# Splitting the first gate's load into idle homes, finer release of buffers, and TensorE's branch turned about

## The reference

```python
h = h + (g_a * y_a + g_b * y_b) @ w_out[l]
hn = rmsnorm(h, norm_ffn_g[l])
# top-1 of 4 groups, then top-2 of the 8 experts in it; combine has 2 weights per token
for e in range(N_EXPERTS):
    h_e = jax.nn.silu(xf @ w_gate[e]) * (xf @ w_up[e])      # 1024 -> 512
    y = y + combine[:, e:e + 1] * (h_e @ w_down[e])         # 512 -> 1024
return rmsnorm(h + y, norm_final_g)
```

## Time and profile before

| what | value |
|---|---|
| median of 3 timed runs | 902.14 us (901.19 to 902.33) |
| profiled execution | 902.81 us |
| its span | 901.07 us |
| granted TensorE clock, mean | 0.979 of full |
| TensorE busy | 853.9 us, 95% |
| DMA | 250.53 MB, mean 278 GB/s |
| chain that ended last | PE 83%, DMA 11%, DVE 3% |

### The profile page before, as it was taken

How to read it: one execution, slowest core, us unless ns; L and a number is a source line. 1 busy time by engine, 2 the same in 40 slices (tenths; PEclk the granted TensorE clock), 3 DMA queues, 4 the chain that set the end, 5 groups by cost and what they waited for, 6 DMA issues and landing times.

```text
span 901.1 us, 11362 instructions
## 1 busy us (share of the span) xinstructions
PE 853.9 (95%) x4613; PEld 551.7 (61%) x4613; DVE 426.4 (47%) x827; ACT 218.8 (24%) x400; POOL 7.5 (1%) x23
## 2 busy tenths in 40 slices
PE   8999999999999999999999967999996799999976
PEld 7888888877777888888734323443542353644632
DVE  5538325677675344436768242434333324335123
ACT  6322222564543222223211111100110100100114
POOL 0000000000000100000000000000000000000000
PEclk9999999999999999999999978999998899999999
DMA  8544212212123733794899999999999999999995
GB/s 296 148 95 117 94 47 94 94 48 94 48 94 84 214 107 94 275 404 162 326 363 420 421 427 425 427 408 423 429 413 428 429 427 426 428 428 426 428 412 198
DMA packets 70887, 250.53 MB, mean 278 GB/s; under 512 B 22792, under 2 KB 46384, under 8 KB 56880
## 3 DMA queue, kind: packets, MB, share of 16 engines
q1 hardware_dynamic: 70320, 248.18, 70.6%
q0 software_dynamic: 432, 1.57, 0.6%
q10 hardware_dynamic: 80, 0.02, 0.0%
HBM read 245.56 MB, written 4.20 MB: 277 GB/s over the span
## 4 chain that ended last, share of the span: by engine, by line
PE 83%; DMA 11%; DVE 3%; issue 1%; ACT 1%; SPq 0%; DVEq 0%; POOLq 0%
PE bank L976 17%; PE bank L670 9%; PE bank L671 9%; PE bank L672 9%; PE bank L1033 8%; DMA R<-w_down 7%; DMA R<-w_gate 3%; PE bank L697 2%; PE bank L698 2%; PE bank L699 2%; PE bank L942 2%; PE by_side L942 2%; PE bank L1020 2%; PE bank L1061 1%; PE bank L1062 1%
## 5 line engine op out<-in xcount | busy, mean ns | idle before, releaser
L976 PE MATMUL bank<-R,packT 128*64 128x512 f32 (+1 forms) x972 | 187.1, 609 | 13.9 <-DMA R<-w_up 7.9
L976 PEld LDWEIGHTS bank<-R,packT 128*64 128x64 f32 (+1 forms) x972 | 59.2, 129 | 123.5 <-issue 122.9
L1544 DVE TENSOR_TENSOR wlo<-raw,whi 128x2048 fp32r<-128x2048 f32 x33 | 75.5, 2287 | 85.2 <-ACT whi L1226 84.7
L670 PE MATMUL bank<-xnT_hi,whi 128*128 128x512 f32 x288 | 113.6, 395 | 0.0
L672 PE MATMUL bank<-xnT_hi,wlo 128*128 128x512 f32 x288 | 112.2, 389 | 0.0
L671 PE MATMUL bank<-xnT_lo,whi 128*128 128x512 f32 x288 | 112.1, 389 | 0.0
L1033 PE MATMUL bank<-R,actT 128*64 128x512 f32 (+1 forms) x384 | 76.0, 653 | 15.3 <-DMA R<-w_down 15.1
L1226 ACT ACTIVATE whi<-raw 128x2048 fp32r<-128x2048 f32 x33 | 63.0, 1909 | 69.0 <-PE by_side L672 33.8
L1033 PEld LDWEIGHTS bank<-R,actT 128*64 128x64 f32 (+1 forms) x384 | 22.9, 137 | 63.3 <-issue 62.6
L672 PEld LDWEIGHTS bank<-xnT_hi,wlo 128*128 128x128 f32 x288 | 54.1, 188 | 11.5
L670 PEld LDWEIGHTS bank<-xnT_hi,whi 128*128 128x128 f32 x288 | 54.1, 188 | 11.3 <-issue 0.6
(11 more groups left out here) (392 smaller groups left out, 1318.2 us busy)
## 6 DMA issues: line engine op xcount, KB each, us to landing
R<-w_up SPq DMA_DIRECT2D x26, 2048.0 KB, 19.6
R<-w_gate SPq DMA_DIRECT2D x25, 2048.0 KB, 20.1
R<-w_down SPq DMA_DIRECT2D x21, 2048.0 KB, 19.4
raw<-w_in SPq DMA_DIRECT2D x17, 1024.0 KB, 5.2
R<-w_down SPq DMA_DIRECT2D x13, 1024.0 KB, 14.4
R<-w_gate SPq DMA_DIRECT2D x9, 1024.0 KB, 7.4
R<-w_up SPq DMA_DIRECT2D x7, 1024.0 KB, 11.0
raw<-w_in SPq DMA_DIRECT2D x20, 256.0 KB, 4.5
```

The lines of the kernel that those rows point to most:

```text
L670: pe.matmul(dst, hi_w, hi_x, start=start, stop=False)
L976: mm = pe.matmul(dst[s * w:(s + 1) * w, :], packT[:, side, c, s * w:(s + 1) * w], part_of(s, c) if part_of else slots[s // 2].tiles[s % 2] ...
L1544: dve.tensor_tensor(wlo[c % 2][:, :], raw[c % 2][:, :], whi[c % 2][:, :].bitcast(F32), ALU.subtract).then_inc(lo_split, 1)
```

## The change

Four things, with no change of what is computed.

1. `first_gate` shrinks to blocks 4 to 7 (8 KB at 16). Blocks 0 and 1 get `gate_head` (4 KB at 214), block 2 `gate_third` (2 KB at 196), block 3 `gate_fourth` (2 KB at 209.5). Some of the router's temporaries change places so that the last one is free in time.
2. Expert 2's up matrix is loaded whole into `R[0]` where half of it was.
3. The releases become finer: after each of the blocks 0 to 5 of the first gate, and after 1, 2, 4 and 6 blocks of the first up projection. The reads of `order` are spread over SP's program.
4. TensorE's program is turned about: the case without overflow is the first branch and holds the whole rest; the case with overflow holds the overflow loop and a second copy of the rest. Round 3's gate waits for one add instead of all; the banks of that spread are taken in another order (bank 0 first); the wait for all adds moves behind the gate.

```diff
-    first_gate = at("first_gate", [P, 8 * DE], F32, 8)
+    first_gate = at("first_gate", [P, 4 * DE], F32, 16)
+    gate_head = at("gate_head", [P, 2 * DE], F32, 214)
+    gate_third = at("gate_third", [P, DE], F32, 196)
+    gate_fourth = at("gate_fourth", [P, DE], F32, 209.5)
...
+        GATE_FIRST = ((0, 2, 3, 5), (6, 7, 1, 2))
+            return GATE_FIRST if line is main and i == OVER_AT - 1 else SPREAD_BANKS
...
-        FIRST_LOADED = (48, 32, 32, 48)
+        FIRST_LOADED = (96, 32, 32, 48)
+        GATE_PARTS = [(c, c + 1) for c in range(6)]
+        UP_PARTS = ((0, 1), (1, 2), (2, 4), (4, 6), (6, 8))
...
-            sp.dma_start(first_gate[:, :], flat(w_gate, 0)).then_inc(slot_loaded[0], 16)
+            sp.dma_start(first_gate[:, :], flat(w_gate, 0)[:, 4 * DE:8 * DE]).then_inc(slot_loaded[0], 16)
             sp.dma_start(first_down[0][:, :], flat(w_down, 0)[:, 0:4 * DE]).then_inc(slot_loaded[2], 16)
-            sp.dma_start(R[0][:, 0:4 * DE], flat(w_up, 2)[:, 0:4 * DE]).then_inc(up_ahead, 16)
+            sp.dma_start(R[0][:, :], flat(w_up, 2)).then_inc(up_ahead, 16)
...
+            sp.wait_ge(hsq_summed, 2 * TT)
+            sp.dma_start(gate_head[:, :], flat(w_gate, 0)[:, 0:2 * DE]).then_inc(slot_loaded[0], 16)
             sp.wait_ge(logits_done, TT)
+            sp.dma_start(gate_third[:, :], flat(w_gate, 0)[:, 2 * DE:3 * DE]).then_inc(slot_loaded[0], 16)
             sp.dma_start(R[6][:, :], flat(w_gate, 2)).then_inc(slot_loaded[3], 16)
+            sp.wait_ge(masks_ready, 1)
+            sp.dma_start(gate_fourth[:, :], flat(w_gate, 0)[:, 3 * DE:4 * DE]).then_inc(slot_loaded[0], 16)
             sp.wait_ge(row_token_ready, 2)
             sp.dma_start(first_down[1][:, :], flat(w_down, 0)[:, 4 * DE:8 * DE]).then_inc(spare_loaded, 16)
...
-            sp.wait_ge(gate_half_done, 1)
-            load_part(4, 0, w_up, 2, 4, 6)
-            load_part(5, 0, w_down, 2, 0, 2)
-            sp.wait_ge(gate_half_done, 2)
-            load_part(4, 0, w_up, 2, 6, 8)
-            load_part(5, 0, w_down, 2, 2, 4)
+            def load_behind_gate(c0, c1):
+                sp.wait_ge(gate_half_done, c1)
+                load_part(5, 0, w_down, 2, c0, c1)
+            for c0, c1 in GATE_PARTS[0:2]:
+                load_behind_gate(c0, c1)
             sp.wait_ge(ordered, 1)
-            quad = [ordered_expert(n) for n in range(4)]
+            quad = {1: ordered_expert(1)}
+            for c0, c1 in GATE_PARTS[2:4]:
+                load_behind_gate(c0, c1)
+            quad[0] = ordered_expert(0)
+            for c0, c1 in GATE_PARTS[4:]:
+                load_behind_gate(c0, c1)
+                load_part(6, 1, w_gate, quad[1], c0 - 4, c1 - 4)
             sp.wait_ge(main.gate_done, 1)
-            load_part(5, 0, w_down, 2, 4, 6)
-            load_part(6, 1, w_gate, quad[1], 0, 4)
...
+            load_part(6, 1, w_gate, quad[1], 2, 4)
+            for n, (c0, c1) in enumerate(UP_PARTS):
+                if c1 < KT:
+                    sp.wait_ge(up_half_done, n + 1)
+                else:
+                    sp.wait_ge(main.up_done, 1)
+                load_part(5, 1, w_down, 3, c0, c1)
+                load_part(6, 0, w_gate, quad[0], c0, c1)
+            quad |= {n: ordered_expert(n) for n in (2, 3)}
             sp.wait_ge(down_half_done, 1)
...
-                    if half_done is not None and (c == KT // 2 - 1 or finer and c == KT // 4 - 1):
+                    if half_done is not None and c + 1 in halves:
...
-                        pe.wait_ge(line.h_added, 8 * i + 1)
+                        pe.wait_ge(line.h_added, 8 * i + spread_banks(line, i)[0].index(2) + 1)
...
+            for i in range(OVER_AT):
+                run_round(i)
+            n_over = pe.value_load(ov_count[0:1, 0:1], min_val=0, max_val=OV_TILES)
+            pe.wait_ge(main.pack_a, 4)
+            pe.wait_ge(main.pack_b, 4)
+            for n in range(2):
+                spread(main, OVER_AT - 1, n, 1 - OVER_AT % 2)
+            def run_rest():
+                pe.wait_ge(main.h_added, 8 * (OVER_AT - 1) + 1)
+                for i in range(OVER_AT, LAST):
+                    run_round(i)
+                finish()
+            with pe.If(n_over < 1):
+                run_rest()
+            with pe.Else():
+                run_overflow()
+                run_rest()
...
+                dve.wait_ge(gate_half_done, 2)
                 make_weights(main, spaced_iota, 0)
```

More of the change, by code:

```diff
@@ L983, in first_gate_part @@
             def first_gate_part(s, c):
-                tile = first_gate if s == 0 else R[1] if c < 6 else gate_rest
-                c = c - 6 if tile is gate_rest else c
-                return tile[:, c * DE:(c + 1) * DE]
+                if s == 0:
+                    tile, c0 = (gate_head, 0) if c < 2 else (gate_third, 2) if c == 2 else (gate_fourth, 3) if c == 3 else (first_gate, 4)
+                else:
+                    tile, c0 = (R[1], 0) if c < 6 else (gate_rest, 6)
+                return tile[:, (c - c0) * DE:(c - c0 + 1) * DE]
             def turn_weights(line, odd):
@@ L1094, in _, with run_round @@
                 turn_fetched(0, n, 2 + n)
-            for i in range(LAST):
+            def run_round(i):
                 odd = i % 2
                 side = odd if i > 2 else 0
[L1098 to L1118, removed]
-                        gather_rows(over, OV_PAIRS // 2 + 1)
-                        pe.wait_ge(over.pack_a, OV_PAIRS + 2)
-                        pe.wait_ge(over.pack_b, OV_PAIRS + 2)
-                    pe.wait_ge(main.h_added, 8 * i)
-                elif i >= 2:
+                if i >= 2 and i != OVER_AT:
                     pe.wait_ge(main.h_added, 8 * (i - 1))
@@ L1132, in _ @@
                     number_rows(2, 2)
-                project(main, slots_of(i, 1), side, bank[1], main.up_done, half_done=up_half_done if i < 2 else None, finer=True)
+                project(main, slots_of(i, 1), side, bank[1], main.up_done, half_done=up_half_done if i < 2 else None,
+                        halves=[c1 for _, c1 in UP_PARTS[:-1]] if i == 0 else (2, 4))
                 if i == 1:
@@ L1166, in _ @@
                     gather_rows(main, i // 2 + 1)
-            last, odd = LAST, LAST % 2
-            pe.wait_ge(main.h_added, 8 * (last - 1))
-            project(main, slots_of(last, 0), odd, bank[0], main.gate_done, packed=None if odd else last + 1)
-            turn_weights(main, odd)
-            for k in range(KT):
-                mm = pe.matmul(bank[1 if k < 4 else 4][:, (k % 4) * P:(k % 4 + 1) * P],
-                               final_gT[:, k:k + 1].to_broadcast([P, P]), ident[:, :], start=True, stop=True)
@@ new lines, in run_overflow @@
+            def run_overflow():
+                pe.wait_ge(main.h_added, 8 * OVER_AT)
+                with pe.Fori(0, OV_PAIRS // 4) as j:
+                    for q in range(4):
+                        o, odd = 4 * j + q, q % 2
+                        if not odd:
+                            gather_rows(over, 2 * j + (q // 2 + 1))
+                        project(over, over_slot(j, q, 0), odd, bank[0], over.gate_done, packed=None if odd else o + 1)
+                        turn_weights(over, odd)
+                        project(over, over_slot(j, q, 1), odd, bank[1], over.up_done)
+                        turn_rows(over, o)
+                        project_down(over, over_slot(j, q, 2), o, None)
+                        for n in range(2):
+                            spread(over, o, n, odd)
+                        pe.wait_ge(over.h_added, 8 * o + 8)
+                gather_rows(over, OV_PAIRS // 2 + 1)
+                pe.wait_ge(over.pack_a, OV_PAIRS + 2)
+                pe.wait_ge(over.pack_b, OV_PAIRS + 2)
@@ L2028, in add_rows @@
                         part = h_tok[:, t, n * 512:(n + 1) * 512]
-                        dve.tensor_tensor(part, bank[SPREAD_BANKS[n][t]][:, :], part, ALU.add).then_inc(line.h_added, 1)
+                        dve.tensor_tensor(part, bank[spread_banks(line, i)[n][t]][:, :], part, ALU.add).then_inc(line.h_added, 1)
             def copy_right(r, b):
```

115 lines of the change are left out of this document (59 added, 56 removed).

## The result

The kernel after takes 906.51 us (median of 8 runs, 904.59 to 980.03) against 902.24 us of the kernel before in the same series (8 runs, 901.19 to 905.29): ratio 1.0042 [1.0029, 1.0055]. It is slower where I forecast faster. (The 980.03 us is one execution at a mean granted clock of 0.842; the ratio leaves it out.) The profiled execution took 904.59 us, its span is 902.8, 1.7 above the 901.1 of before.

The account below looks back on a forecast made before the run. The end was taken as the weight stream's end plus a fixed tail. Early part 1.2 us (1.7 - 0.5) plus holes 1.7 us gave 2.9 us: 899.9 us profiled, 899.2 us median, range 897.9 to 901.6.

Parts of the forecast that it names:

- The loads fit the hole, and gate_fourth was in time: Ahead of the first gate: four blocks, 2.46 us of stream, fill the hole at 442 to 446; gate_fourth lands by 447.9.
- I take 0.5 us, near the lower row, since the queue ahead is short: First row gather, started at 443.79: delayed 0.5 us by weight loads in flight until about 445.2; bounds 0 and 4.1 us.
- The gain is capped at 1.7 us: At the 471.14 load, behind 1.7 us of backlog: a stream 1.96 us ahead runs dry, so the early gain stops there.
- Behind this place the reserve grows: After the 471 load the queue lengthens: the load of 509.79 has 14 us of queue before it.
- VectorE's new wait: Ahead of make_weights: met at about 451.8, VectorE arrives at 452.32, so it costs nothing, with 0.5 us to spare.
- The branch: TensorE's 6105 ns branch at 547.0 becomes 0.1 us; round 3's gate starts 3.8 us earlier at full clock, TensorE 6.8 us earlier.
- The holes of 594 to 600 and 656: Low-traffic windows from late-freed buffers close with earlier issues: 1.7 us gained, bounds 0 and 2.4.
- C: Rival: first gather queued behind new loads lands after 8.8 us, first gate 4.1 us late; 902.8 us, slower; chance 0.06.
- The packet rule: First gather could wait behind a gate-load packet, then share with first_down: 1.3 us delay instead of 0.5, sum 0.8 us less.

Follow-up runs that it names:

- ahead_only: Kernel before plus three loads, 1 MB in all, that nobody uses, issued where gate_head, gate_third and gate_fourth stand; 907.55 us, 1.0055.
- ahead_down_later: ahead_only with first_down's second half issued only when the first gather has landed; 903.26 us, 1.0010 of the kernel before.
- half_behind: Kernel after with blocks 4 to 7 of expert 2's gate (1 MB) issued behind first_down's second half; 901.53 us, 0.9988 of the kernel before.
- the mended versions: Kernels after with loads moved behind first_down's second half or held until the gather landed, some with other releases; 0.9985 to 1.0001 of the kernel before.
- wait_only: Kernel before with the other bank order and the moved waits, TensorE's branch left as it was; 902.50 us, 0.9999.
- branch_only: Kernel before with TensorE's program turned about, the other bank order and the moved waits, no new load; 902.08 us, 0.9985.
- changed_again: Kernel after, unchanged, run again in a later series; 906.32 us, 1.0036 of the kernel before.
- half_coarse: half_behind with first-round releases by two blocks (gate) and by 2, 2 and 4 (up); 902.68 us, 0.9993 of the kernel before.

## Why the prediction was wrong, point by point

**The loads fit the hole, and gate_fourth was in time: right.** It was issued at 440.64 and took 7.3 us, which is 447.9. The four blocks did move ahead: +0.99 MB by 450.

**"I take 0.5 us, near the lower row, since the queue ahead is short": wrong.** This is the step that failed. The gather took 7.82 us instead of 4.7, 3.1 more; started 0.8 us earlier, it put the gate 2.35 us late. The 0.5 us priced the queue ahead of the gather (1.4 us of traffic) and left out the load behind it; `first_down` stood only in the sentence with 1.3 us beside the sum. ahead_only against ahead_down_later puts 0.45% of the time on that load. What the trace of before showed on it, 33 GB/s at 444 to 446 while a 1 MB load had been issued, I read as a hole to be filled and not as the gather's cover. The measured 3.1 lay inside my bounds of 0 and 4.1, and near the end that I had not taken: the row of 8.8 us, a gather beside a full stream, was the nearer one.

**A term that the sum didn't have: the clock.** A pause of 3.8 us on TensorE ahead of the first gate; the waits of the kernel after (line waited for: us, times, longest) show it in their third line:

```profile
PE bank L1055 <- DMA R<-w_down: 15.5, 2, 8.9
PE bank L996 <- DMA R<-w_up: 11.9, 1, 11.9
PE bank L953 <- DMA rows<-hn_rows,row_token: 3.8, 1, 3.8
```

Before, that line was 0.7. Behind the pause the granted clock is 0.55 and 8.70 us go into a 7.09 us projection: 1.6 us. I had the price in hand, 10.08 against 7.04 behind the branch's pause, and used it only for what the branch would win.

**"The gain is capped at 1.7 us": moot, and the lead is worth less than that.** With the gate's end 3.93 us late, and as many blocks issued by then as before, the lead of 2.5 us was spent first, and the stream then starved. The load expected to land in 5.1 us (471.14 before, issued at 475.09 after) took 6.0. half_behind shows the lead with the gather in order: 0.85 MB ahead at 460, 0.14 MB at 490, summed from the same windows. "Behind this place the reserve grows" was wrong: the landing of 509.79 has a long queue, but between it and 471 lies a second dry spot at 480 to 484, behind the release of the second half of the down matrices. That the branch part alone gives 0.9985 and the mended versions of the whole change 0.9985 to 1.0001 leaves the early part nothing that can be told from zero.

**VectorE's new wait: costs nothing, but with no slack.** I had 0.5 us to spare for a gate on time. With the late gate at half clock VectorE stands 2.45 us:

```profile
455.99 0.41 DVE L1959 TENSOR_SCALAR weight_a<-spaced_iota,small 128x256 f32<-128x256 f32 x1 [2.45 <-PE bank L996]
...
460.08 0.42 DVE L1966 TENSOR_TENSOR weight_a<-weight_a,weight_b 128x256 f32<-128x256 f32 x1
```

The last of the weights is done at 460.50, the gate at 461.02: hidden by 0.5 us.

**The branch: right.** The row of the changed kernel (duration ns min/median/max, first and last start):

```profile
L1252 PEldq COMPARE_BRANCH  x2: 86/1696/3307, 550.8 to 891.6; - x2
```

The 6105 ns have become 86, the gate runs at full clock right behind the spread, and wait_only shows that in the kernel before it was the jump that held it. The new jump at the end starts at 891.6, while the last matmuls still run (the last ends at 894.1), and is over at 894.9, under the rest of the tail.

**The holes of 594 to 600 and 656: right.** I forecast 1.7 us; 0.80 MB are 1.9 us of stream, and branch_only's ratio is worth 1.4 us. Its interval of 0.4 to 2.3 us holds all three.

**The rivals.** C is what happened. Its mechanism (the gather lands at the third one's pace, the chain to 471 moves, the lead is no help) is there step by step. I gave it 4.1 us of late gather and 902.8 us in all; it got 3.1 us, plus the clock's 1.6, and 906.5. Without the pause of the clock C stopped short of the threshold that I had set for it, and I gave it 0.06 on the ground that the gather had little traffic ahead: the argument that failed. What the sum of C lacked is also that the starved stream loses the lead and the delay both. The profiled execution is 1.7 us longer in span, the medians are 4.3 apart: the gather's start and length differ from one execution to the next (443.02 and 7.82 here, 444.39 and 7.93 in changed_again), and the profiled one is the quickest of its series.

**The packet rule.** I had weighed 1.3 us for the gather from the Trainium skill (DMA: Bandwidth & Descriptors, Queues, rings and completion order), by which engines take packets from the queues in turn. The trace agrees with taking turns: in the kernel after, both queues move bytes in each microsecond from 2 to 7 behind the gather's issue. But 1.3 us was too little by 1.8: it counted one packet and a short stretch of sharing with `first_down`, and the sharing lasted until the gather's end. How many packets a turn takes, no run here shows.

**Open.** Why the last lines of the gather are still slow in some executions of the mended versions; and how the 4.3 us between the medians divide exactly between gather, clock and the dry spots.

## What to carry to other kernels

Before you fill a hole in a queue, ask who uses it: a small transfer on the critical path, issued from another queue, may owe its speed to it, and the load issued behind that transfer counts as much as the bytes ahead. A delay ahead of TensorE is to be priced with the clock that may follow the pause. A compare-and-branch that jumps over a long body is worth turning about so that the common case falls through, with the remaining jump at the end of TensorE's program; here the wait that stood behind the old jump was moved as well.

## What the runs showed of the hardware that was not expected

- The gather of the first rows (0.53 MB) takes 4.3 to 4.4 us with the queue thinned out and no load issued until it has landed, 5.2 us with 1 MB ahead and none behind (ahead_down_later), and 4.5 to 5.6 us when the next 1 MB load follows 1.2 us behind it on a queue that has run low. With a full queue ahead and that load behind it takes 6.9 to 7.9 us (four executions of three kernels). One execution with the queue run low took 8.47 us (half_coarse): its last 0.03 MB were caught by the next load.
- TensorE's taken jump lasts 6.1 to 6.4 us in the middle of the full weight stream (6105, 6388 and 6408 ns in three kernels) and 3.3 us at the end, when the stream has ended (3307 and 3267 ns). Not taken, the same instruction takes 86 ns. In these runs the place in the program and the traffic changed together, so which of them makes the difference is not shown.
- After the pauses ahead of the first gate (2.8 us in ahead_only, 3.8 us in the kernel after) and behind the old jump (3.9 us in the kernel before) the granted clock was 0.50 to 0.55 of full, the 1.2 GHz level, and the projection behind took 8.06 (half_coarse, behind 4.4 us) to 10.08 us instead of 7.04 to 7.09. But round 3's gate of ahead_only ran at 1.00 and took 7.09 us behind a pause of 3.9 us: the length of the pause alone doesn't tell it.
